# Index keys and head weights as one 72-row product tile, the keys' second copy made by an on-chip transfer

## What is computed

```python
proj = rms_norm_2(x, g_pre_mix[l]) @ w_in[l]
u_pool, q, k, v, iq, ik, iw = jnp.split(proj, SPLIT_POINTS, axis=-1)
iq = rope_partial(iq.reshape(B, S, IDX_HEADS, IDX_DIM), positions, IDX_ROPE_DIM)
ik = rope_partial(ik[:, :, None, :], positions, IDX_ROPE_DIM)[:, :, 0, :]
iw = iw * (IDX_HEADS ** -0.5)
...
logits = jnp.einsum('bqhd,bsd->bqhs', iqb, ik32) * (IDX_DIM ** -0.5)
score = jnp.einsum('bqh,bqhs->bqs', iwb, jax.nn.relu(logits))
score = jnp.where(allowed[None], score, -jnp.inf)
top_val, top_idx = lax.top_k(score, topk)
```

## Time and profile before

| | |
|---|---|
| median of 3 runs | 2648.98 us (2646.34 to 2650.09) |
| the profiled execution | 2649.76 us, its span 2648.0 us |
| mean granted TensorE clock | 0.962 |
| PE busy | 2436.3 us, 92% of the span |
| DVE busy | 1516.7 us, 57% |
| ACT busy | 835.7 us, 32% |
| POOL busy | 350.3 us, 13% |
| products (L323) on the chain that ended last | 16% of the span |

### The profile page before, as it was taken

How to read it: one execution, slowest core, us unless ns; L and a number is a source line. 1 busy time by engine, 2 the same in 40 slices (tenths; PEclk the granted TensorE clock), 3 DMA queues, 4 the chain that set the end, 5 groups by cost and what they waited for, 6 DMA issues and landing times. The chain is left out here.

```text
span 2648.0 us, 29239 instructions
## 1 busy us (share of the span) xinstructions
PE 2436.3 (92%) x11390; PEld 1955.5 (74%) x11398; DVE 1516.7 (57%) x2122; ACT 835.7 (32%) x1155; POOL 350.3 (13%) x219
## 2 busy tenths in 40 slices
PE   7988999998998899999888897999979889899996
PEld 5866888887786688888765676888856567688885
DVE  6774544455687445445478856444447984744544
ACT  4454222233435322223232343222223234322221
POOL 1011000000201100001024512000022541200002
PEclk9999999999999999999889998999989999899998
DMA  4211222221221132222121211222212111122222
GB/s 146 104 49 58 92 91 99 105 96 67 92 88 64 48 112 96 95 95 96 48 88 50 78 37 60 100 101 100 89 55 89 64 64 48 62 98 96 95 95 79
DMA packets 33301, 217.75 MB, mean 82 GB/s; under 512 B 4128, under 2 KB 4384, under 8 KB 7840
## 3 DMA queue, kind: packets, MB, share of 16 engines
q1 hardware_dynamic: 33184, 216.18, 23.1%
HBM read 214.07 MB, written 2.10 MB: 82 GB/s over the span
## 5 line engine op out<-in xcount | busy, mean ns | idle before, releaser
L323 PE MATMUL ps<-gh,wh 128*128 128x512 f32 (+1 forms) x1728 | 699.3, 405 | 109.3 <-DVE gl L464 65.4
L323 PE MATMUL ps<-gl,wh 128*128 128x512 f32 (+1 forms) x1728 | 681.9, 395 | 0.0
L323 PE MATMUL ps<-gh,wl 128*128 128x512 f32 (+1 forms) x1728 | 681.6, 394 | 0.0
L307 ACT ACTIVATE wh<-wr 128x2048 fp32r<-128x2048 f32 x196 | 374.0, 1908 | 560.2 <-PE ps L323 560.0
L313 DVE TENSOR_TENSOR wl<-wr,wh 128x2048 fp32r<-128x2048 f32 x172 | 394.8, 2295 | 248.9 <-ACT wh L307 248.9
L323 PE MATMUL ps<-hh,wh 128*128 128x512 f32 x1280 | 504.7, 394 | 7.4 <-DVE hl L944 3.1
L323 PE MATMUL ps<-hh,wl 128*128 128x512 f32 x1280 | 499.8, 390 | 0.0
L323 PE MATMUL ps<-hl,wh 128*128 128x512 f32 x1280 | 499.3, 390 | 0.0
L323 PEld LDWEIGHTS ps<-gh,wh 128*128 128x128 f32 (+1 forms) x1728 | 328.7, 190 | 211.0 <-DVE gl L464 72.7
L323 PEld LDWEIGHTS ps<-gl,wh 128*128 128x128 f32 (+1 forms) x1728 | 328.4, 190 | 72.8 <-issue 5.3
L323 PEld LDWEIGHTS ps<-gh,wl 128*128 128x128 f32 (+1 forms) x1728 | 328.0, 190 | 72.0
(11 more groups left out here) (204 smaller groups left out, 2414.4 us busy)
## 6 DMA issues: line engine op xcount, KB each, us to landing
wr<-in_weights SPq DMA_DIRECT2D x198, 1024.0 KB, 4.7
x<-in_xt SPq DMA_DIRECT2D x1, 2048.0 KB, 11.8
out_yt<-x SPq DMA_DIRECT2D x1, 2048.0 KB, 7.2
tmp<-in_positions SPq DMA_DIRECT2D x4, 256.0 KB, 3.3
arena<-in_gates SPq DMA_DIRECT2D x2, 512.0 KB, 4.8
arena<-in_embed SPq DMA_DIRECT2D x2, 512.0 KB, 5.6
par<-in_params_b SPq DMA_DIRECT2D x2, 274.0 KB, 3.1
par<-in_params_a SPq DMA_DIRECT2D x2, 157.5 KB, 2.7
```

The lines of the kernel that those rows point to most:

```text
L307: act.activation(mem.wh[:, c % 2, :], mem.wr[:, c % 2, :], ACT.Copy).then_inc(sem["high"], 1)
L323: done = pe.matmul(out, stationary, moving, start=(first and n == 0), stop=(last and n == 2), skip_group_check=True)
```

## The change

The index key stands once in chunk 2 and the 8 head weights directly behind it, so tile 4 has 72 rows (`IKW`): 64 of the key, 8 of the weights. Tile 5 of before is gone, and all later tiles have a number less by one. VectorE now takes the head weights first, from partitions 64 to 71, and rotates the key on 64 partitions. The end of this rotation raises `ik_ready`. SP waits for it behind the load of chunk 5 and copies the 64 rows to partitions 64 to 127 of `ik`, a transfer from on-chip memory to on-chip memory, which raises `ik_doubled`. TensorE waits for that ahead of the first logits. The transposes wait for `drained` to be 5, where they waited for 6.

```diff
-def rotate(dve, steps, mem, sem, tile, out, cos, sin, width=P):
+def rotate(dve, steps, mem, sem, tile, out, cos, sin, width=P, done=None):
...
-    steps.mark(dve.tensor_tensor(out, out, mem.tmp[0:width, 2, :], ALU.add))
+    last = dve.tensor_tensor(out, out, mem.tmp[0:width, 2, :], ALU.add)
+    if done is None:
+        steps.mark(last)
+    else:
+        last.then_inc(done, 1)
...
-B_TILE = {c: 2 * c for c in range(B_V)}
-B_TILE.update({B_V: 18, B_V + 1: 22})
+B_TILE = {0: 0, 1: 2, B_IKW: 4}
+B_TILE.update({c: 2 * c - 1 for c in range(B_U, B_V)})
+B_TILE.update({B_V: 17, B_V + 1: 21})
...
+IKW = DH + HEADS2
...
                 for c in range(2, B_FF):
                     chunk(c)
+                    if c == 5:
+                        sp.wait_ge(sem["ik_ready"], 1)
+                        sp.dma_start(ik[DH:P, :], ik[0:DH, :]).then_inc(sem["ik_doubled"], 16)
...
-                rotate(dve, own, mem, sem, 4, ik, cos, sin)
-                dve.wait_ge(sem["product"], 6)
+                dve.wait_ge(sem["product"], B_TILE[B_IKW] + 1)
                 dve.wait_ge(sem["spread"], 1)
                 own.settle()
-                dve.tensor_tensor(tmp[0:HEADS2, 3, :], ps[0:HEADS2, 5 % 4, :], mem.rb[0:HEADS2, :], ALU.mult)\
-                    .then_inc(sem["drained"], 1)
+                own.mark(dve.tensor_tensor(tmp[DH:IKW, 3, :], ps[DH:IKW, 0, :], mem.rb[DH:IKW, :], ALU.mult))
+                rotate(dve, own, mem, sem, B_TILE[B_IKW], ik[0:DH], cos, sin, DH, sem["ik_ready"])
...
-                product_tile(pe, mem, sem, B_IKW, 0, 4, mem.gh, mem.gl)
-                product_tile(pe, mem, sem, B_IKW, P, 5, mem.gh, mem.gl, width=HEADS2)
+                product_tile(pe, mem, sem, B_IKW, 0, B_TILE[B_IKW], mem.gh, mem.gl, width=IKW)
                 linear_chunk(3, mem.gh, mem.gl)
 
-                pe.wait_ge(sem["drained"], 6)
+                pe.wait_ge(sem["drained"], B_TILE[B_IKW] + 1)
...
+                    if s == 0:
+                        pe.wait_ge(sem["ik_doubled"], 16)
...
-        ikw[:, 0:64], ikw[:, 64:128], ikw[:, 128:136] = ik, ik, iw
+        ikw[:, 0:64], ikw[:, 64:72] = ik, iw
```

More of the change, by code:

```diff
@@ L1210, in first_stack_layer @@
         clear(nc, used)
-B_TILE = {c: 2 * c for c in range(B_V)}
-B_TILE.update({B_V: 18, B_V + 1: 22})
-B_TILE.update({B_POOL: 26, B_POOL + 1: 30, B_ATT: 34, B_ATT + 1: 38})
-B_TILE.update({c: 42 + 2 * (c - B_FF) for c in range(B_FF, B_CHUNKS + 1)})
+B_TILE = {0: 0, 1: 2, B_IKW: 4}
+B_TILE.update({c: 2 * c - 1 for c in range(B_U, B_V)})
+B_TILE.update({B_V: 17, B_V + 1: 21})
+B_TILE.update({B_POOL: 25, B_POOL + 1: 29, B_ATT: 33, B_ATT + 1: 37})
+B_TILE.update({c: 41 + 2 * (c - B_FF) for c in range(B_FF, B_CHUNKS + 1)})
+IKW = DH + HEADS2
 B2_QK, B2_V, B2_CR, B2_U, B2_IQ, B2_IK, B2_SC, B2_MB = 0, 4096, 6144, 7168, 9280, 11328, 11840, 13376
@@ L1270, in second_stack_layer @@
             "scored maxed exped scaled_done turned untangled weighted pair_high pair_low updated branch_scaled added zeroed hidden hidden_high "
-            "hidden_low padded pool_own"))
+            "hidden_low padded pool_own ik_ready ik_doubled"))
         with nc.Block() as block:
@@ L1495, in _ @@
                 dve.wait_ge(sem["padded"], 1)
-                drain_u(6)
-                drain_u(7)
+                drain_u(B_TILE[B_U])
+                drain_u(B_TILE[B_U] + 1)
                 dve.wait_ge(sem["weights_turned"], 1)
@@ L1534, in picks @@
                         rounds[0] += 1
-                drain_u(8)
+                drain_u(B_TILE[B_U] + 2)
                 picks(1)
-                drain_u(9)
+                drain_u(B_TILE[B_U] + 3)
                 picks(3)
@@ L1711, in _ @@
                 first_two_chunks(pe, mem, sem, 0, 0, 0, gained(0))
-                product_tile(pe, mem, sem, B_IKW, 0, 4, mem.gh, mem.gl)
-                product_tile(pe, mem, sem, B_IKW, P, 5, mem.gh, mem.gl, width=HEADS2)
+                product_tile(pe, mem, sem, B_IKW, 0, B_TILE[B_IKW], mem.gh, mem.gl, width=IKW)
                 linear_chunk(3, mem.gh, mem.gl)
-                pe.wait_ge(sem["drained"], 6)
+                pe.wait_ge(sem["drained"], B_TILE[B_IKW] + 1)
                 for i in range(QT):
-                    last = pe.transpose(ps[:, 5, HEADS2 * i:HEADS2 * (i + 1)], tmp[0:HEADS2, 3, P * i:P * (i + 1)], ident[0:HEADS2, 0:HEADS2])
+                    last = pe.transpose(ps[:, 5, HEADS2 * i:HEADS2 * (i + 1)], tmp[DH:IKW, 3, P * i:P * (i + 1)], ident[DH:IKW, DH:IKW])
                 last.then_inc(sem["weights_turned"], 1)
```

## The result

The changed kernel took 2655.24 us, median of 10 runs (2649.9 to 2656.54), against 2648.31 us for the kernel before beside it (10 runs, 2645.12 to 2650.09): ratio 1.0025, 95% interval 1.0015 to 1.0034. It is slower by 6.9 us. The time lies in the range of the forecast, 2643 to 2656, and 4.6 us above its value of 2650.6. The likeliest outcome on record was no change, at 0.65; slower had 0.15.

What follows compares the result with a forecast made beforehand. TensorE's chain up to the second stack's first logits was taken to bound; per layer -5.5 tile, +0.75 chunk 3's low half, +4.25 rotation and copy wait, +1.3 clock gave +0.8, so 2648.98 + 1.6 = 2650.6 us, range 2643 to 2656.

Steps and rivals of the forecast that it cites:

- What bounds: Second stack: TensorE holds the chain up to the logits, and everything behind the last logits moves with their start.
- The tile: The 8-row tile's 24 passes at 0.228 us leave TensorE: 5.5 us a layer, 11.0 us in all.
- Chunk 3's low half: Behind tile 4, TensorE waits for VectorE to make this half, which the 8-row tile had covered: 0.75 us a layer.
- The rotation with GpSimd in its way: Ahead of the logits, GpSimd's low half of chunk 4 still stretches a VectorE addition to some 4.9 us, only earlier.
- the addition that gets in first: Rival, chance 0.12: tile 2's addition on VectorE precedes GpSimd's start, logits start 2.5 us earlier a layer, 2643.9 us.
- GpSimd that holds up nothing: Rival, chance 0.13: GpSimd's low half delays nothing the keys need, 4.65 us a layer gained, 2639.7 us.
- The idle time on VectorE: Before the last rotation VectorE idled 0.35 us longer than before the others, unexplained; a part was taken, giving 2037.7.
- The copy: SP's 128 KB on-chip transfer of the keys ahead of the logits takes 2.05 us, range 1.4 to 4.4.
- The clock: TensorE's idle time before the logits drops its clock to 0.50 for 3.3 us, costing 1.3 us a layer (0 to 1.65).
- the forecast's own line of 5.3 us: 0.2%, 5.3 us, was taken as about what a measurement of this kernel can tell from no change.
- The forecast's own case: Chance 0.60: the GpSimd delay moves up and the copy takes the rest, 2650.6 us, by itself 2646 to 2654.
- a transfer of 4.4 us: Slower rival, chance 0.13: the copy is as late as the 4 KB load, logits 1.85 us late, 2656.0 us.

Runs made afterwards that it cites:

- e7_all_parts: The changed kernel with the second copy on ScalarE, chunk 4's low half on VectorE, chunk 3's a rotation earlier and first logits ahead of chunk 4's wait: 2636.65 us.
- e9_early3_transfer: The changed kernel with chunk 4's low half on VectorE, chunk 3's low half one rotation earlier and the transfer kept: 2640.62 us, ratio 0.9977.
- e2_low4_vector: The changed kernel with chunk 4's low half made by VectorE behind the keys' rotation, not by GpSimd: 2640.09 us, ratio 0.9972.
- e5_filled: The changed kernel with 18 unread matmuls in TensorE's idle time, 5 ahead of the transposes' wait and 13 behind: 2646.95 us, ratio 0.9999.
- e1_scalar_copy: The changed kernel with the second copy of the keys made by ScalarE and not by a transfer: 2646.81 us, ratio 0.9997.

## Why the prediction was right, and where it was off

*What bounds.* Right. The shift at the end of the logits is carried through: behind the last logits of the first layer the kernel after is 3.9 us late in its profile (1.1 of it from before the logits), and at the masks of that layer, 90 us on, still 3.9.

*The tile.* Right: 5.5 us a layer forecast, 5.4 us seen where nothing takes its place (e7_all_parts).

*Chunk 3's low half.* 0.75 us was put down as a term. The idle time was 0.47 us, and a term it was not: e9_early3_transfer took it away for nothing, because the transfer comes later. The sum was not hurt, since it held the wait for the transfer as the remainder.

*The rotation with GpSimd in its way.* Right in place and size: GpSimd's low half began 9.34 us after the first shuffle (2026.1 - 2016.84 = 9.3 was forecast), and the addition of tile 2 took 5.02 us. Of the two rivals there, the addition that gets in first did not happen, by 0.12 us, and GpSimd that holds up nothing, at 2639.7, is what e2_low4_vector made true: 2640.09.

*The idle time on VectorE.* It came back as 0.49 us, ahead of the head weights; I had taken 0.1 us of it. In the kernels of the experiments it is there as well, with 0.47 to 0.50 us, ahead of the instruction behind the fourth rotation, whichever that is. Its cause I did not find. These 0.4 us more than I took are most of why the logits did not start the forecast's 0.5 us early.

*The copy.* 2.05 us from the line through two loads; 2.20 us measured, with an issue 0.03 us after the addition's end in place of 0.18. The two errors of mine cancel: 2.37 us from the end of the addition (2042.52) to the first logits, 2.35 forecast. By the price of the Trainium skill (DMA: Bandwidth & Descriptors, "Anatomy of one DMA") the transfer was an estimated 2.3 us; the measured 2.20 us lies between that and my 2.05. The section's price is a fit for transfers that GpSimd issues, and SP issued this one. The logits were to start 0.5 us early and started 0.03 us early.

*The clock.* This is the step that failed, and by its size: "I take 1.3 us a layer, and keep 0 and 1.65". That it would fall was right. The price came from one stretch of 3.3 us at half clock, after 3.54 us of idle time, and I used its length as the most that an idle time of this kind can cost. The stretch behind ours is twice as long, 6.8 us with 16 or 17 records, and costs 2.8 us; filled, it costs nothing (e5_filled). Nor is one row a safe price. In the kernel after, the same idle time ahead of the pool mix comes back, 3.56 us in place of 3.54, and TensorE then runs at 0.50 for 5.1 us in place of 3.3, with the clock at 0.50 already at the end of the wait:

```profile
1482.80:1487.90 5.10, 5.08 (x18) 0.50 0.00 0
```

The rival in which the addition gets in first counted on an idle time too short for the clock to fall; e1_scalar_copy, with 1.24 and 1.66 us, shows that this was not safe either.

With 2.8 us in place of 1.3 and 0 in place of the 0.5 gained, the forecast's own sum gives 2 x 2.8 = 5.6 us, and 2648.3 + 5.6 = 2653.9 us against 2655.24. The remaining 1.3 us stays open. It is more than the medians of the kernel before beside the runs differ by (2647.56 to 2648.31), but the interval of the change, 1.0015 to 1.0034 or 4 to 9 us, takes 5.6 us in.

*The range and the chances.* By the forecast's own line of 5.3 us the outcome is slower, to which it gave 0.15. That the time still lies in the range is in part luck. The forecast's own case was to end at 2654; the range went on to 2656 only for a transfer of 4.4 us, which did not come. Slower stood at 0.15 because the forecast needed a transfer of over 3.4 us for it (3.6 by its own terms: 5.3 / 2 - 1.65 = 1.0 us late). A clock term with a fair upper end would have put much of the forecast's 0.60 beyond 5.3 us.

## What to carry to other kernels

Work taken from the busiest engine is worth only what the next thing in line leaves: list every signal that this engine waits for behind the piece, each with the time at which it comes, before you count the piece. A piece that looks wasted can cover a wait, and keep TensorE's clock up; here 24 passes of 8 rows hid a rotation, a low half on GpSimd and could have hidden a transfer. When the gap is closed by moving the work that made it, the whole gain comes (11.3 us measured, two tiles of 5.4 by the trace), and when it is only filled with matmuls that nobody reads, the loss at least goes away.

## What I had not expected of the hardware

- The slow stretch behind an idle time of 3.2 us was 6.8 us, with 3.22 us idle alone as with 1.24 us ahead of it. After 1.24 and 1.66 us it was about half of that. In the kernel before one behind 3.54 us took only 3.3 us, and in the kernel after the same place had 5.1 us of it behind the wait. Idle time of the same length is not followed by the same stretch; take the longest seen as the upper bound. And one idle time of 2.74 us left the clock at 1.00, where 1.24 and 1.66 us with four small transposes between did not, so the longest idle time alone does not tell whether the clock falls.
- ScalarE copied 64 x 512 values from partitions 0 to 63 to partitions 64 to 127 in 0.63 us, against 2.20 us for the transfer. The trace of e1_scalar_copy has it:

```profile
2034.18 0.63 ACT L1370 ACTIVATE arena<-arena 64x512 f32<-64x512 f32 x1 [12.16 <-DVE arena L503]
```
